# Layer entry after an expert loop: first weight panels taken from the loop's prefetch, the loop's last scatters moved in among the memory transposes

## The chip, the cores and the metric

The kernel runs on one core of one Trainium2 chip. The metric is the device time of one execution in microseconds (us); the time given for a kernel is the median of its runs. A profiled execution has a time of its own and a span, from the first to the last instruction that the profiler saw. The engines are named as in the profile: PE (TensorE, the matrix engine), DVE (VectorE), ACT (ScalarE), POOL (GpSimd), and SP (SyncE), which here only issues DMA transfers. Each runs its own instruction list in order, and they wait for one another by semaphores.

## What is computed

Two blocks follow each other on a sequence of 256 tokens of width 1024, all in float32. The first block ends in a layer whose feed-forward part is a mixture of 8 experts; its output is the residual `h` of the second block, two layers of a hybrid of attentions. Cut to what the change touches:

```python
def moe_swiglu(h, router, we_gate, we_up, we_down):      # end of the first block
    gates = ...                                          # softmax over the 2 best of 8 experts
    out = jnp.zeros_like(h)
    for e in range(N_EXPERTS):
        out = out + gates[..., e:e + 1] * swiglu(h, we_gate[e], we_up[e], we_down[e])
    return out

def hybrid_layer(x, mem, ...):                           # second block, twice
    h = rms_norm_2(x, g_mix)
    z = h @ w_in
    ...
    kv = (rms_norm_2(mem, g_mem) @ w_mkv)                # keys and values of the memory
    ...
    x = x + y @ w_o
    hm = rms_norm_2(x, g_mlp)
    return x + jnp.square(jax.nn.relu(hm @ w_up)) @ w_down
```

The 256 tokens are 2 tiles of 128. The 256 rows of `mem` do not depend on the first block.

## The kernel before, in words

**Panels.** All weights are streamed in panels of 128 x 1024 float32 (512 KB). Each product is made of three matmuls, so every panel is split: ACT writes the rounded part `whi` (`split_to`, line 556), DVE the rest `wlo` (line 1016). `whi` and `wlo` have 4 slots (`SLOTS`). Both engines keep a count of the panels split (`hi`, `lo`), PE a count of those used. The activations are split in the same way: PE transposes 4 tiles of 128 x 128 into one of two PSUM banks `TB` (`turn_group`, line 1898, called a turn below), ACT copies the bank out as the high part (line 591), DVE computes the low part (line 1064) and thereby frees the bank (`tfree`). Eight tiles in depth, four turns, make one operand for 256 tokens.

**The expert loop** (from about 480 us to 1468.5 us of the trace) does 8 jobs, one for each entry of a job table that DVE computes from the router (`tab`, lines 1509 to 1513); an entry is the number of an expert. SP streams a job's 84 panels from the array `wm` into a ring of 7 slots called `deep`; after the last panel of a job it loads the first 7 panels of the next job's expert, the "follower". The last job has a follower too: its table entry is the last expert, and nobody uses those 7 panels. A job ends with two chunks of 14 panels (`KE // 2`), which leave two halves of the job's output in PSUM; ACT and DVE split each into `outhi` and `outlo` (lines 865 and 1615, count `s_ol`). The output is scattered back to the tokens by 4 matmuls a half (`scatter`, line 2222, into the banks SC0 and SC1) and added to `h` by DVE (`add_scattered`, line 1572, two instructions a half, count `s_h`). In the loop this is done within the next job. For the last job it stands behind the loop.

**The entry of the hybrid layer** (`Walk(e, B)`, l = 0 and 1). The first chunk of a layer computes the memory's keys and values: 4 panels of 12 matmuls each, whose other operand is the transposed `mbuf` (the memory rows, scaled long before) in `chi` and `clo`. Four turns of `mbuf` feed it (`turn_rows`, `turned`). During its panels 2 and 3 the first two turns of `h` are made for the next chunk (`early`), with the other two to follow (`late`). The weights of this block come from an array `w2` into the ring `raw` of 4 slots. `raw` and `deep` lie on the same memory: slots 0 to 3 of `deep` are the 4 slots of `raw`, and slots 4 to 6 lie on `qkT`, which is written later in the layer.

What stands between the loop and the first panel, for l = 0: DVE adds both halves to `h`, then releases everything with six drains (`B.lo` for SP, `B.free`, `B.tfree`, `B.sfree`, `B.ofree`, `s_res` for PE), copies the norm gains (`n2`, line 1635, count `s_par`) and splits 3 panels before it comes to its part of the turns. PE waits for `s_res` and `s_par` before its first turn. SP waits for the 7 unused panels and for `B.lo`, then loads panel 0 of `w2`. ACT splits 3 panels, which wait for these loads, and only then copies out the first turn. `n2` is a table of 24 gains per layer; PE waits for `s_par` in the second layer too, and `chi` and `clo` lie on memory that the loop's `outhi` and `selT` and the feed-forward part's `fhi` and `flo` use.

Of the kernel before, what the change touches and what calls it, by code (L numbers as in the profile page):

```python
# [59 lines left out]
PER_TURN = {k: TURN * v for k, v in PER_JOB.items()}  # L60
PER_LAYER = dict(p=PANELS_B, g=30, t=16, n=2, h=0, s=16, a=6, r=16, v=8, o=6, u=6, k=10, va=0)
# [58 lines left out]
def build(nc, d):  # L120
    ctx = ExitStack()
    with ctx:
# [208 lines left out]
        class Walk:  # L331

            def __init__(self, e, s, chain=None):
                self.e, self.s, self.chain = e, s, chain
                self.key = "va" if chain is s.va else "vd"
                self.n = dict.fromkeys(PER_JOB, 0)
                self.split = 0
                self.ring = s.ring
                self.it, self.per = None, None

# [71 lines left out]
        def _(e):  # L412
# [41 lines left out]
            with e.Fori(0, turns) as it:  # L454
                for x in range(TURN):
                    expert = e.value_load(tab[0:1, bass.ds(it * TURN + (x + 1), 1)], min_val=0, max_val=NE - 1)
                    for p in range(DEEP, PANELS_M):
                        expert_panel(expert, p, p % DEEP, it * (TURN * PANELS_M) + (x * PANELS_M + p - DEEP + split))
                    follower = e.value_load(tab[0:1, bass.ds(it * TURN + (x + 2), 1)], min_val=0, max_val=NE - 1)
# [5 lines left out]
            with e.Fori(0, 2 * PANELS_B // SLOTS - 1) as k:  # L465
                for i in range(SLOTS):
                    e.wait_ge(B.lo, k * SLOTS + (SLOTS + i + 1))
                    e.dma_start(raw[:, i, :], d["w2"][bass.ds(k * SLOTS + (SLOTS + i), 1)].rearrange("a p n -> p (a n)")
                                ).then_inc(B.raw[i], 16)
# [72 lines left out]
        def _(e):  # L542
            act = nc.scalar.activation

            def split_to(w, target):

                while w.split < target:
# [5 lines left out]
                    e.wait_ge(loaded[slot], base if w.it is None else w.it * (16 * w.per["p"] // depth) + base)  # L553
# [451 lines left out]
        def _(e):  # L1005
            v = nc.vector

            def split_to(w, target):

                while w.split < target:  # L1010
                    p = w.split
                    w.split += 1
                    q = p + 1
                    slots, loaded, first = w.ring
                    e.wait_ge(w.s.hi, q if w.it is None else w.it * w.per["p"] + q)
                    v.tensor_tensor(wlo[:, p % SLOTS, :], slots[:, (p - first) % len(loaded), :], whi[:, p % SLOTS, :].bitcast(F32),  # L1016
                                    ALU.subtract).then_inc(w.s.lo, 1)
# [474 lines left out]
            for t in range(T):  # L1492
# [16 lines left out]
            w.link(v.tensor_tensor(tmp[:, :, 0:NE - 1], jobs_c[:, :, 0:NE - 1],  # L1509
                                   end.unsqueeze(1).to_broadcast(wide)[:, :, 0:NE - 1], ALU.is_ge))  # L1510
            v.tensor_scalar(R[:, 1041:1042], end[:, NE - 1:NE], TURN + 0.5, 1.0, ALU.is_gt, ALU.add)
            w.link(v.reduce_sum(R[:, 1042:1042 + MAXJOB], tmp[:, :, 0:NE - 1], axis=AX.X))
# [54 lines left out]
            def add_scattered(c, it, x):  # L1567

                e.wait_ge(s_scat, it * (2 * TURN) + (2 * x + c + 1))
                for t in range(T):  # L1570
                    x = h[:, t, c * 512:(c + 1) * 512]
                    i = v.scalar_tensor_tensor(x, SC[t][:, :], jobcur[:, 1, t:t + 1], x, ALU.mult, ALU.add)
# [48 lines left out]
            for c in range(2):  # L1621
                add_scattered(c, turns, 0)

            e.drain().then_inc(B.lo, SLOTS)
            e.drain().then_inc(B.free, 2)
            e.drain().then_inc(B.tfree, 2)
            e.drain().then_inc(B.sfree, 4)
            e.drain().then_inc(B.ofree, 2)
            e.drain().then_inc(s_res, 4)  # L1630
            w = Walk(e, B, B.vd)
            for l in range(2):
# [4 lines left out]
                split_to(w, LOOK)  # L1637
                turned(w, lambda k: n2[:, k:k + 1], (chi, clo))
# [173 lines left out]
        def _(e):  # L1812
# [405 lines left out]
            def scatter(c):  # L2218

                for t in range(T):  # L2220
                    for q, y in enumerate((outhi, outlo)):
                        i = mm(SC[t][:, :], selT[:, t, :], y[:, c, :], start=(q == 0), stop=(q == 1))  # L2222
# [57 lines left out]
            w = Walk(e, B)  # L2280
            for l in range(2):
                w.layer(l)
                e.wait_ge(s_par, l + 1)
                rows, ahead = turn_rows(w, mbuf, (A.nhn, 1)), early(w, h, (s_res, l * 4 + 3 + (l == 0)))

                def entry(panel):
                    rows(panel)
# [3 lines left out]
                chunk_tokens(w, chi, clo, FULL, before=entry)  # L2291
# [234 lines left out]
```

## Time and profile before

| | us |
|---|---|
| median of 3 runs | 2293.86 |
| lowest and highest | 2292.74, 2295.32 |
| the profiled execution's own time | 2297.4 |
| its span | 2295.5 |
| PE busy in the span | 2219.1 (97%) |
| DVE busy | 1726.7 (75%) |
| ACT busy | 1411.3 (61%) |
| mean of PE's granted clock | 0.984 of full |

The profile's page gives busy time by engine, a band of 40 slices, the chain of work that ended last, and the costliest groups. With PE busy 97% of the span, what is to be read is where PE is not busy, or busy at half its clock. The views with times of their own (the chain in order of time, the timeline of one engine, the table of stretches) count from the start of the span. Matmuls overlap: a row's length is that of one in the pipeline (0.39 us), while their starts stand 0.23 us apart.

### The profile page before, as it was taken

To read this page: it belongs to the slowest core of one execution; us is meant where nothing else is said; L and a number is where in the kernel's file an instruction comes from. 1 tells how busy PE (TensorE), PEld (TensorE's weight loads), DVE (VectorE), ACT (ScalarE), POOL (GpSimd) and SP (SyncE) were. 2 spreads that over 40 slices of the span, in tenths; PEclk is the share of its full clock that TensorE was granted. 3 is DMA by queue.
4 is the path that set the end of the run, shared out by engine and by line. 5 is a ranking of instruction groups with operands and counts; after the bars stand their busy time and mean duration, and the time that the engine had idled before them with its cause. 6 is when DMAs were issued, how large, how long until landed. Compare 5 with 4: busy or idle time off the path is not lost.

```text
span 2295.5 us, 36562 instructions
## 1 busy us (share of the span) xinstructions
PE 2219.1 (97%) x11818; PEld 1893.7 (82%) x11818; DVE 1726.7 (75%) x2308; ACT 1411.3 (61%) x1901; POOL 109.6 (5%) x113
## 2 busy tenths in 40 slices
PE   8999998999999999999999999799989999998998
PEld 7889986778888888888888888687879878887987
DVE  7856656588998989898989899666576546657654
ACT  4264445467887878777877778545545434564543
POOL 8300005000000000000000000000000000000000
PEclk9999998999999999999999999899999999999999
DMA  6235553269999999999999999754445555434554
GB/s 225 74 129 184 184 192 120 74 215 374 345 367 356 359 358 356 349 361 345 365 344 365 362 352 374 275 183 138 134 162 191 186 181 174 147 129 165 194 185 146
DMA packets 152640, 557.79 MB, mean 243 GB/s; under 512 B 16912, under 2 KB 17040, under 8 KB 152336
## 3 DMA queue, kind: packets, MB, share of 16 engines
q1 hardware_dynamic: 152032, 554.53, 67.5%
q8 instruction: 97, 1.59, 0.3%
q10 hardware_dynamic: 432, 1.02, 0.1%
q14 instruction: 79, 0.65, 0.1%
HBM read 554.44 MB, written 1.05 MB: 242 GB/s over the span
## 4 chain that ended last, share of the span: by engine, by line
PE 85%; issue 7%; DVE 4%; ACT 3%; DMA 1%; POOL 0%; DVEq 0%; ACTq 0%; SPq 0%; POOLq 0%
PE L L1830 59%; PE L L1883 10%; PE L L2316 5%; PE TB L1898 2%; PE L L1847 2%; PE SC L2061 1%; PE SC L2213 1%; PE L L2001 1%; PE SC L2222 1%; DVE wlo L1016 1%; ACT SMX L652 1%; PE SC L1968 1%; PE L L2111 1%; ACT whi L556 0%; DVE hn L1746 0%
## 5 line engine op out<-in xcount | busy, mean ns | idle before, releaser
L1016 DVE TENSOR_TENSOR wlo<-deep,whi 128x1024 fp32r<-128x1024 f32 x675 | 795.5, 1221 | 58.9 <-ACT whi L556 38.4
L556 ACT ACTIVATE whi<-deep 128x1024 fp32r<-128x1024 f32 x675 | 706.5, 1060 | 139.8 <-PE L L1830 135.5
L1016 DVE TENSOR_TENSOR wlo<-raw,whi 128x1024 fp32r<-128x1024 f32 x368 | 446.0, 1227 | 275.0 <-ACT whi L556 268.8
L556 ACT ACTIVATE whi<-raw 128x1024 fp32r<-128x1024 f32 x368 | 383.1, 1058 | 332.8 <-PE L L1830 191.0
L1830 PE MATMUL L<-whi,xhi 128*128 128x512 f32 (+1 forms) x1200 | 474.8, 396 | 8.7 <-DVE wlo L1016 4.8
L1830 PE MATMUL L<-whi,xlo 128*128 128x512 f32 (+1 forms) x1200 | 467.8, 390 | 0.0
L1830 PE MATMUL L<-wlo,xhi 128*128 128x512 f32 (+1 forms) x1200 | 467.7, 390 | 0.0
L1830 PEld LDWEIGHTS L<-whi,xhi 128*128 128x128 f32 x1200 | 226.7, 189 | 57.9 <-DVE wlo L1016 8.8
L1830 PEld LDWEIGHTS L<-whi,xlo 128*128 128x128 f32 x1200 | 226.5, 189 | 48.0
L1830 PEld LDWEIGHTS L<-wlo,xhi 128*128 128x128 f32 x1200 | 226.7, 189 | 44.7
L1830 PE MATMUL L<-whi,mhi 128*128 128x512 f32 x448 | 175.9, 393 | 0.0
L1830 PE MATMUL L<-wlo,mhi 128*128 128x512 f32 x448 | 174.5, 390 | 0.0
L1830 PE MATMUL L<-whi,mlo 128*128 128x512 f32 x448 | 174.4, 389 | 0.0
L1883 PE MATMUL L<-x2hi,whi 128*128 128x256 f32 x512 | 145.0, 283 | 0.0
L1883 PE MATMUL L<-x2hi,wlo 128*128 128x256 f32 x512 | 144.9, 283 | 0.0
L1883 PE MATMUL L<-x2lo,whi 128*128 128x256 f32 x512 | 144.9, 283 | 0.0
L1883 PE MATMUL L<-xhi,whi 128*128 128x256 f32 x448 | 127.4, 284 | 1.4 <-DVE xlo L1064 0.8
L1883 PE MATMUL L<-xlo,whi 128*128 128x256 f32 x448 | 126.8, 283 | 0.0
L1883 PE MATMUL L<-xhi,wlo 128*128 128x256 f32 x448 | 126.8, 283 | 0.0
L486 POOL TENSOR_TENSOR stat<-stat,halfneg 128x2 f32<-128x2 f32 (+3 forms) x18 | 21.6, 1198 | 2121.8 <-DVE stat L1038 1907.9
L1830 PE MATMUL L<-whi,fhi 128*128 128x512 f32 x280 | 109.3, 390 | 1.4 <-DVE wlo L1016 1.4
L1830 PE MATMUL L<-wlo,fhi 128*128 128x512 f32 x280 | 109.0, 389 | 0.0
(327 smaller groups left out, 3414.7 us busy)
## 6 DMA issues: line engine op xcount, KB each, us to landing
deep<-wm SPq DMA_DIRECT2D x679, 512.0 KB, 5.6
raw<-w SPq DMA_DIRECT2D x368, 512.0 KB, 4.0
mbuf<-mem SPq DMA_DIRECT2D x2, 1024.0 KB, 8.4
const<-const SPq DMA_DIRECT2D x1, 1312.0 KB, 7.7
out<-hn SPq DMA_DIRECT2D x2, 512.0 KB, 2.6
h<-x ACTq DMA_DIRECT2D x1, 512.0 KB, 4.9
h<-x SPq DMA_DIRECT2D x1, 512.0 KB, 4.8
mbuf<-gfin SPq DMA_DIRECT2D x1, 512.0 KB, 4.4
```

The lines of the kernel that those rows point to most:

```text
L556: act(whi[:, p % SLOTS, :], slots[:, slot, :], ACT.Copy).then_inc(w.s.hi, 1)
L652: ins = act(s, s, ACT.Exp, bias=top[:, 2 * x + t:2 * x + t + 1], scale=-1.0, accum_out=den[:, 2 * x + t:2 * x + t + 1])
L1016: v.tensor_tensor(wlo[:, p % SLOTS, :], slots[:, (p - first) % len(loaded), :], whi[:, p % SLOTS, :].bitcast(F32), ALU.subtract).then_inc( ...
L1830: i = mm(L[2 * (g % 2) + t][:, 0:width], x[:, k, row], y[:, slot, cols], start=(k == k0 and q == 0), stop=(k == k0 + n - 1 and q == 2))
L1847: i = mm(L[2 * (g % 2) + t][:, :], x[:, k, t * P:(t + 1) * P], y[:, slot, kk * 512:(kk + 1) * 512], start=(k == 0 and q == 0), stop=(k == ...
L1883: i = mm(out, x[:, slot, cols], y[:, k, :], start=(k == 0 and q == 0 and f % 2 == 0), stop=(k == KD - 1 and q == 2 and f % 2 == 1), skip_g ...
L1898: i = tr(TB[w.n["t"] % 2][:, c:c + P], src, ident)
L1968: ins = mm(bank(w, x)[:, t * S:t * S + c], qkT[half, qp, t * P:(t + 1) * P], key[half, 0:c], start=True, stop=True)
L2001: ins = mm(out(w, w.n["o"])[:, at:at + HD], PT[:, w.n["v"] % 2, x, kt * S + t * P:kt * S + (t + 1) * P], parts[j][2](x, kt), start=(j == 0 ...
L2061: ins = mm(SC[c % 2][:, f * S:(f + 1) * S], diag[2 * c + f][:, i, :], u[:, 2 * c + f, tap:tap + S], start=(i == 0), stop=(i == TAPS_PE - 1))
L2111: i = mm(L[2 * ((w.n["g"] + c) % 2) + t][:, :], x[:, k, row], y[:, slot, kk * 512:(kk + 1) * 512], start=(k == 0 and q == 0), stop=(k == K ...
L2316: i = mm(L[2 * (bank % 2) + t][:, :], x[:, k, t * P:(t + 1) * P], y[:, slot, kk * 512:(kk + 1) * 512], start=(k == 0 and q == 0), stop=(k ...
```

## The change

1. **Prefetch.** `w2` is appended to `wm` (`W2` is where it begins), and the job table counts over all 8 experts instead of 7, so that an entry behind the last job is 8: the follower of the last job is the first 7 panels of the hybrid block. SP no longer waits for `s_deep` nor loads panels 0 to 6 of `w2`; it goes on with panel 7 into `raw` slot 0 when panel 0 has been split. ACT and DVE read panels 0 to 6 from `deep` (`led`, `lead`).
2. **Final scatters.** `scatter(0)` goes into SC0 and SC1 as before but waits only for the first half of the output, `scatter(1)` into L2 and L3, two banks of the matmul accumulators. PE no longer waits for DVE's addition between them; it makes turns 0 and 1 of the memory rows between the two, and turn 2 behind them.
3. **Order on DVE and ACT.** DVE releases `B.lo`, `B.tfree` and one count of `B.free` straight behind the loop; then it splits one panel, does its part of a turn, and adds half 0; one more panel, one more turn, half 1; then the third panel and the turns 2 and 3; the other drains come behind. ACT splits one panel before each of the first three turns. ACT's first split now waits for `s_par`.
4. **Buffers and waits.** The memory rows' operand is written to `x2hi` and `x2lo` instead of `chi` and `clo`, in both layers; PE's wait for `s_par` is gone in both layers, ACT's wait for `s_h` as well.

```diff
-                    expert = e.value_load(tab[0:1, bass.ds(it * TURN + (x + 1), 1)], min_val=0, max_val=NE - 1)
+                    expert = e.value_load(tab[0:1, bass.ds(it * TURN + (x + 1), 1)], min_val=0, max_val=NE)
...
-            for i in range(DEEP):
-                e.wait_ge(s_deep[i], turns * (TURN * 16 * PANELS_M // DEEP) + 16)
-            panels(B, lambda i: d["w2"][i], SLOTS)
+            def later_panel(i, panel, split):
+
+                e.wait_ge(B.lo, split)
+                e.dma_start(raw[:, i, :], d["wm"][bass.ds(panel, 1)].rearrange("a p n -> p (a n)")).then_inc(B.raw[i], 16)
+
+            rest = 2 * PANELS_B - DEEP - SLOTS
+            for i in range(SLOTS):
+                later_panel(i, W2 + DEEP + i, SLOTS + i + 1)
...
ACT, layer entry
-            w = Walk(e, B, B.va)
+            w = Walk(e, B, B.va).led(turns)
...
-                split_to(w, LOOK)
                 e.wait_ge(s_par, l + 1)
-                turned(w, lambda k: n2[:, k:k + 1], chi)
-                e.wait_ge(s_h, turns * (2 * TURN) + 8)
+                e.wait_ge(w.s.used, w.at("p", SLOTS))
+                for q in range(4):
+                    if l == 0:
+                        split_to(w, min(q + 1, LOOK))
+                    turned_group(w, q, lambda k: n2[:, k:k + 1], x2hi)
...
DVE, behind the loop
-            for c in range(2):
-                add_scattered(c, turns, 0)
-
-
             e.drain().then_inc(B.lo, SLOTS)
-            e.drain().then_inc(B.free, 2)
             e.drain().then_inc(B.tfree, 2)
-            e.drain().then_inc(B.sfree, 4)
-            e.drain().then_inc(B.ofree, 2)
-            e.drain().then_inc(s_res, 4)
-            w = Walk(e, B, B.vd)
+            e.drain().then_inc(B.free, 1)
+            w = Walk(e, B, B.vd).led(turns)
...
-                split_to(w, LOOK)
-                turned(w, lambda k: n2[:, k:k + 1], (chi, clo))
+                for q in range(4):
+                    if l == 0:
+                        split_to(w, min(q + 1, LOOK))
+                    turned_group(w, q, lambda k: n2[:, k:k + 1], (x2hi, x2lo))
+                    if l == 0 and q < 2:
+                        add_scattered(q, turns, 0, (SC, L[2:4])[q])
+                        if q == 0:
+                            e.drain().then_inc(s_res, 3)
+                if l == 0:
+                    e.drain().then_inc(B.free, 1)
+                    e.drain().then_inc(B.sfree, 4)
+                    e.drain().then_inc(B.ofree, 2)
+                    e.drain().then_inc(s_res, 1)
...
PE, behind the loop
-            e.wait_ge(s_ol, turns * (2 * TURN) + 2)
+            e.drain().then_inc(B.used, SLOTS)
+            e.wait_ge(s_ol, turns * (2 * TURN) + 1)
             e.wait_ge(s_xj, turns * (TURN * 4) + 4)
             scatter(0)
-            e.wait_ge(s_h, turns * (2 * TURN) + 7)
-            scatter(1)
-
-
-            e.wait_ge(s_res, 4)
-            e.drain().then_inc(B.used, SLOTS)
+            w = Walk(e, B)
+            w.layer(0)
+            e.wait_ge(A.nhn, 1)
+            turn_group(w, mbuf, 0)
+            turn_group(w, mbuf, 1)
+            e.wait_ge(s_ol, turns * (2 * TURN) + 2)
+            scatter(1, L[2:4])
+            turn_group(w, mbuf, 2)
             e.drain().then_inc(B.rcopy, 2)
             e.drain().then_inc(B.pv, 2)
...
-                chunk_tokens(w, chi, clo, FULL, before=entry)
+                chunk_tokens(w, x2hi, x2lo, FULL, before=entry)
```

What stands in a row on the engines, printed from the built programs. In these rows `TB0` and `TB1` are the banks of the turns, `const` the identity, `b_thi` says that ACT has copied the turn out, `b_hi` that ACT has split the panel, `s_scat` that PE has scattered.

DVE from the end of the loop (line 1615, or 1637 after, splits the last half of the last job's output) in the kernel before:

```order
L1615 TENSOR_TENSOR outlo_64<-L0,outhi_63 128x512 [waits s_oh,a_free]
...
L1572 SCALAR_TENSOR_TENSOR h_54<-SC0,jobcur_102,h_54 128x512 [waits s_scat]
...
L1635 COPY n2_99<-small_95 128x24
L1016 TENSOR_TENSOR wlo_53<-raw_49,whi_52 128x1024 [waits b_hi,s_par]
L1016 TENSOR_TENSOR wlo_53<-raw_49,whi_52 128x1024 [waits b_hi] x2
L1064 SCALAR_TENSOR_TENSOR clo_68<-TB0,n2_99,chi_67 128x256 [waits b_thi]
```

And DVE from the same place in the changed kernel:

```order
L1637 TENSOR_TENSOR outlo_64<-L0,outhi_63 128x512 [waits s_oh,a_free]
...
L1650 COPY n2_99<-small_95 128x24
L1039 TENSOR_TENSOR wlo_53<-deep_51,whi_52 128x1024 [waits b_hi,s_par]
L1087 SCALAR_TENSOR_TENSOR x2lo_88<-TB0,n2_99,x2hi_87 128x256 [waits b_thi]
...
L1594 SCALAR_TENSOR_TENSOR h_54<-SC0,jobcur_102,h_54 128x512 [waits s_scat]
...
L1039 TENSOR_TENSOR wlo_53<-deep_51,whi_52 128x1024 [waits b_hi]
L1087 SCALAR_TENSOR_TENSOR x2lo_88<-TB1,n2_99,x2hi_87 128x256 [waits b_thi]
...
L1594 SCALAR_TENSOR_TENSOR h_54<-L2,jobcur_102,h_54 128x512 [waits s_scat]
```

The additions moved from ahead of the first panel's split to behind the first and the second turn, and the split reads `deep` instead of `raw`.

PE from the last job's scatters to the first matmul of the layer in the kernel before:

```order
L2222 MATMUL SC0<-outhi_63,selT_104 128x512 [waits s_xj]
...
L2222 MATMUL SC0<-outhi_63,selT_104 128x512 [waits s_h]
...
L1898 MATMUL TB0<-const_96,mbuf_75 128x128 [waits s_res,b_tfree,a_nhn,s_par]
...
L1898 MATMUL TB1<-const_96,mbuf_75 128x128 [waits b_tfree]
...
L1898 MATMUL TB0<-const_96,mbuf_75 128x128 [waits b_tfree]
...
L1830 MATMUL L0<-whi_52,chi_67 128x512 [waits b_lo,b_tfree,b_free]
```

And PE there in the changed kernel:

```order
L2248 MATMUL SC0<-outhi_63,selT_104 128x512 [waits s_xj]
...
L1924 MATMUL TB0<-const_96,mbuf_75 128x128 [waits b_tfree,a_nhn]
...
L1924 MATMUL TB1<-const_96,mbuf_75 128x128 [waits b_tfree]
...
L2248 MATMUL L2<-outhi_63,selT_104 128x512 [waits s_ol]
...
L1924 MATMUL TB0<-const_96,mbuf_75 128x128 [waits b_tfree]
...
L1856 MATMUL L0<-whi_52,x2hi_87 128x512 [waits b_lo,b_tfree,b_free]
```

The second scatter no longer waits for `s_h`, DVE's addition of the first half, and two turns stand ahead of it; the wait for `s_res` and `s_par` is gone.

## Rows read from the trace of the kernel before

**Rows 1.** Table of stretches: busy per engine (instructions), granted PE clock, DMA share, GB/s.
```profile
800.00:1000.00 200.00, 199.96 (x935) 166.15 (x934) 183.83 (x199) 158.31 (x188) 0.00 (x0) 1.00 0.95 355
...
1468.50:1502.30 33.80, 20.87 (x81) 16.18 (x81) 16.55 (x25) 12.21 (x20) 0.00 (x0) 0.70 0.47 163
...
1886.50:1903.50 17.00, 13.96 (x61) 11.53 (x62) 8.33 (x15) 6.03 (x12) 0.00 (x0) 0.80 0.19 66
```
**Rows 2.** Chain that ended last around the first entry: start us, us, what.
```profile
1437.10 31.41 PE L L1830 x138
...
1469.41 0.70 DVE outlo L1615
...
1470.22 1.20 PE SC L2222 x4
...
1472.91 2.09 PE SC L2222 x4
...
1477.44 6.02 DMA raw<-w
...
1483.48 1.06 ACT whi L556
...
1484.57 1.23 DVE wlo L1016
...
1486.63 1.12 PE TB L1898 x4
1487.75 5.07 PE L L1830 x12
1492.82 0.44 PE TB L1898 x4
1493.25 2.77 PE L L1830 x12
```
**Rows 3.** Timeline of DVE at the first entry: start, us, line, op, [idle before <-releaser].
```profile
1475.02 1.41 DVE L1572 SCALAR_TENSOR_TENSOR h<-SC,jobcur,h 128x512 f32<-128x512 f32 x2 [2.17 <-PE SC L2222]
1477.01 0.18 DVE L1635 COPY n<-small 128x24 f32<-128x24 f32 x1 [0.58 <-issue]
...
1494.16 0.88 DVE L1064 SCALAR_TENSOR_TENSOR clo<-TB,n,chi 128x256 fp32r<-128x256 f32 x2 [4.63 <-ACT chi L591]
```
**Rows 4.** Timeline of ACT at the first entry.
```profile
1487.79 0.84 ACT L591 ACTIVATE chi<-TB,n 128x256 fp32r<-128x256 f32 x2 [1.80 <-PE TB L1898]
```
**Rows 5.** Timeline of PE: first matmul of panel 0, first matmul of panel 4.
```profile
1487.40 0.78 PE L1830 MATMUL L<-whi,chi 128*128 128x512 f32 x1
...
1502.30 0.39 PE L1830 MATMUL L<-whi,xhi 128*128 128x512 f32 x1
```
**Rows 6.** Table of stretches, the first entry cut where the granted clock changes.
```profile
1468.50:1472.90 4.40, 1.18 (x4) 0.67 (x4) 3.00 (x4) 0.60 (x1) 0.00 (x0) 0.91 0.45 180
...
1486.60:1492.60 6.00, 5.97 (x16) 4.79 (x17) 1.64 (x4) 0.84 (x2) 0.00 (x0) 0.50 0.40 117
1492.60:1502.30 9.70, 9.70 (x50) 7.99 (x48) 5.84 (x9) 6.15 (x10) 0.00 (x0) 1.00 0.30 108
```
**Rows 7.** The loop's loads into `deep`: the last issues, and issue to landing.
```profile
1441.08 24.84 SPq L445 DMA_DIRECT2D deep<-wm  x19
...
DMA to landing us min/median/max: 3.1/5.6/7.4
```
**Rows 8.** Waits of ACT from 600 to 1440 us: total us, times, longest.
```profile
ACT whi L556 <- DMA deep<-wm: 3.8, 9, 0.7
```
**Rows 9.** Chain that ended last around the second layer's entry.
```profile
1888.16 0.19 DVE n L1635
...
1889.50 0.85 ACT chi L591 x2
...
1891.38 1.12 PE TB L1898 x4
1892.50 4.16 PE L L1830 x12
```
**Rows 10.** The same place in PE's timeline, and a stretch of it.
```profile
1888.39 1.84 PE L1898 MATMUL TB<-const,mbuf 128*128 128x128 f32 x8 [1.93 <-DVE n L1635]
...
1891.38:1895.40 4.02, 4.02 (x12) 3.35 (x13) 1.60 (x4) 0.84 (x2) 0.00 (x0) 0.50 0.02 4
```
**Rows 11.** Timeline of DVE, first instruction inside the expert loop.
```profile
479.26 1.22 DVE L1016 TENSOR_TENSOR wlo<-deep,whi 128x1024 fp32r<-128x1024 f32 x1 [1.14 <-issue]
```

More of the change, by code:

```diff
@@ L338, in __init__, with led @@
                 self.ring = s.ring
+                self.lead = None
                 self.it, self.per = None, None
+            def led(self, turns):
+                self.lead = turns * (16 * PER_TURN["p"] // DEEP) + 16
+                self.ring = (raw, self.s.raw, DEEP)
+                return self
             def at(self, kind, plus=0):
@@ L552, in split_to @@
                     slot, base = (p - first) % depth, 16 * ((p - first) // depth + 1)
-                    e.wait_ge(loaded[slot], base if w.it is None else w.it * (16 * w.per["p"] // depth) + base)
+                    if w.lead is not None and p < DEEP:
+                        slots, slot = deep, p
+                        e.wait_ge(s_deep[p], w.lead)
+                    else:
+                        e.wait_ge(loaded[slot], base if w.it is None else w.it * (16 * w.per["p"] // depth) + base)
                     q = p + 1
@@ L1014, in split_to @@
                     slots, loaded, first = w.ring
+                    slot = (p - first) % len(loaded)
+                    if w.lead is not None and p < DEEP:
+                        slots, slot = deep, p
                     e.wait_ge(w.s.hi, q if w.it is None else w.it * w.per["p"] + q)
-                    v.tensor_tensor(wlo[:, p % SLOTS, :], slots[:, (p - first) % len(loaded), :], whi[:, p % SLOTS, :].bitcast(F32),
+                    v.tensor_tensor(wlo[:, p % SLOTS, :], slots[:, slot, :], whi[:, p % SLOTS, :].bitcast(F32),
                                     ALU.subtract).then_inc(w.s.lo, 1)
@@ L2216, in gather, with scatter @@
                         i.then_inc(s_gat, 1)
-            def scatter(c):
+            def scatter(c, banks=SC):
                 for t in range(T):
                     for q, y in enumerate((outhi, outlo)):
-                        i = mm(SC[t][:, :], selT[:, t, :], y[:, c, :], start=(q == 0), stop=(q == 1))
+                        i = mm(banks[t][:, :], selT[:, t, :], y[:, c, :], start=(q == 0), stop=(q == 1))
                 i.then_inc(s_scat, 1)
@@ L2268, in _ @@
                 w.end("pgt")
-            e.wait_ge(s_ol, turns * (2 * TURN) + 2)
+            e.drain().then_inc(B.used, SLOTS)
+            e.wait_ge(s_ol, turns * (2 * TURN) + 1)
             e.wait_ge(s_xj, turns * (TURN * 4) + 4)
             scatter(0)
-            e.wait_ge(s_h, turns * (2 * TURN) + 7)
-            scatter(1)
-            e.wait_ge(s_res, 4)
-            e.drain().then_inc(B.used, SLOTS)
+            w = Walk(e, B)
[6 more added lines that the diff above has]
+            turn_group(w, mbuf, 2)
             e.drain().then_inc(B.rcopy, 2)
             e.drain().then_inc(B.pv, 2)
-            w = Walk(e, B)
             for l in range(2):
-                w.layer(l)
-                e.wait_ge(s_par, l + 1)
-                rows, ahead = turn_rows(w, mbuf, (A.nhn, 1)), early(w, h, (s_res, l * 4 + 3 + (l == 0)))
+                if l == 1:
+                    w.layer(l)
+                    for q in range(3):
+                        turn_group(w, mbuf, q)
+                ahead = early(w, h, (s_res, l * 4 + 3))
                 def entry(panel):
-                    rows(panel)
+                    if panel == 1:
+                        turn_group(w, mbuf, 3)
+                    e.wait_ge(w.s.tfree, w.at("t", max(panel - 1, 0)))
                     if panel == 3:
```

22 lines of the change are left out of this document (11 added, 11 removed).

## The prediction

> **What bounds the kernel now.** I read the table of stretches first. In the expert loop PE is busy for all of its time at full clock, and so nothing can be won there except by less PE work [rows 1]. In the 33.8 us after it, 1468.5 to 1502.3, PE is busy 20.9 us at a mean clock of 0.70, and in the 17 us at the second layer's entry 14.0 us at 0.80 [rows 1]. The change touches these two places. The chain of waits, read second, tells what fills the first: the split of the last half, scatter, addition, scatter, addition, then the load of a panel (6.02 us), its split on ACT (1.06) and DVE (1.23), a turn, and panel 0 at half clock (5.07 where panel 1 takes 2.77) [rows 2]. Panel 0 starts at 1487.40 and panel 4, the first of the next chunk, at 1502.30 [rows 5]. From panel 4 on PE's work and order are the same in both kernels, so the gain of this entry is how much earlier panel 4 starts. The six drains and the copy of the gains take from 1476.43 (1475.02 + 1.41) to 1477.19 [rows 3].
>
> **The load goes.** The 7 panels that the loop fetches last are now the ones needed. Their last issue is near 1465.9 (1441.08 + 24.84) and a load of this ring lands within 7.4 us [rows 7], by 1473.3 at worst; panel 0, six issues of 1.38 us earlier (24.84 over 18), is there when the loop ends. SP has nothing on the path any more: panel 7 is asked for when panel 0 is split, and is needed after seven panels of 2.77 us [rows 2]. Seven loads of 256 are saved, which PE does not notice. The longer count in the job table adds 17 elements to two small DVE instructions; I cost it at nothing.
>
> **The new chain, step by step.** T = 1468.51 is the end of the loop's matmuls (1437.10 + 31.41), and DVE ends the last split at 1470.11 (1469.41 + 0.70) [rows 2]. Both stay.
> - DVE then has three drains and the copy. Six drains took 0.58 us; three take 0.3 to 0.6, with the copy 0.18 [rows 3]: 1470.8.
> - ACT waits for this copy (`s_par`, the new wait) with the split of panel 0 and all later panels behind it, and DVE in turn waits for ACT. 1.06 us: 1471.9. Its copy of turn 0 takes 0.84 [rows 4]: 1472.75. PE has made turns 0 and 1 by then, from 1470.4 on, and both scatters.
> - DVE splits panel 0 (1.23) to 1473.2 and does turn 0 (0.88 [rows 3]) to 1474.1. This releases PE's turn 2; the first matmul followed such a turn's start by 0.77 us (1487.40 against 1486.63) [rows 2, 5]. Panel 0 starts at 1474.9, against 1487.4: 12.5 us earlier.
> - From here DVE is the slow one, as the additions now lie among its turns. It goes on: addition 1.41, a drain 0.1, split 1.23, turn 1 0.88, to 1477.7; addition 1.41, split 1.23, turn 2 0.88, to 1481.25; turn 3 0.88, four drains 0.4, split 1.23, first turn of `h` 0.88, to 1484.6; split and second turn of `h` 2.1, to 1486.7.
> - PE: panel 1 needs turn 1, panel 2 turn 2, panel 3 the first turn of `h`, panel 4 the second. Each takes a turn of 0.44 and 2.77 [rows 2].
>
> **The clock decides the last us.** In the first entry before, the clock was full through the first scatter (1.20 us for 4) and half in the second (2.09 for 4), after PE had been idle 1.7 and 1.5 us [rows 2, 6]. At the second entry it was half at the first turns after an idle 1.93 us [rows 10]. In the changed kernel PE is idle some 0.9 us ahead of the turns and 1.8 us behind the second scatter, much like that, so I take the half clock (1.2 GHz of 2.4) for the start of panel 0. It came back 6.0 us after PE resumed at the first entry [rows 6] and 4.0 us after at the second [rows 10]. With 4.0 from 1474.1, panel 0 has 7.5 matmuls at 0.43 us and 4.5 at 0.23, and ends at 1479.1; with 6.0 it ends at 1480.1. Then panels 1, 2 and 3 follow at 3.2 us each (PE is now later than DVE): 1482.4, 1485.6, 1488.8, or 1483.3, 1486.5, 1489.7. Panel 4 starts at 1488.8 to 1489.7 instead of 1502.3: 12.6 to 13.5 us won. I take **13.1**.
>
> **The second layer.** PE's turns no longer wait for the gains. What is left is that ACT starts when the gains are copied, at 1888.4 (1888.16 + 0.19), instead of 1889.50 behind PE's first turn [rows 9]: **1.1 us**. The additions that end the layer stay ahead of the copy. Bounds: nothing, if ACT is slow to start, and 2.5 us if the turns, now straight behind the last matmul, also save the slow clock of panel 0 (4.16 against 2.77 us, 1.4 [rows 2, 9]). Other buffers (`x2hi` for `chi`) have the same shape, and the tables of waits show no reader of them in these stretches: zero. Nothing in the 384 us behind each entry changes; all loads there are covered, so I let the gain pass whole to the end.
>
> **Sum.** 13.1 + 1.1 = 14.2. The profiled execution of 2297.4 us would become 2283.2. It stood 3.5 us over the median of the runs, 2293.86, so the median becomes **2279.7**, a gain of 0.62%.
>
> **Rivals.**
> - *The clock stays full.* Then DVE's chain sets the pace: panel 1 starts at 1478.1, panel 2 at 1481.7, panel 3 at 1485.0, panel 4 at 1487.8. That is 14.5 us, with 1.1 to 2.5 in the second layer 15.6 to 17: 2276.9 to 2278.3. For it: PE has turns and a scatter in a stretch where it idled before. Against it: the two idle times of the same length that did end in half clock. Chance 0.25.
> - *Leaving the loop stalls.* Behind the loop ACT and DVE had slack before that would hide a slow first instruction: DVE waited 1.35 us for the scatter, ACT far longer. Now both stand on the path at once. At the loop's entry DVE's first instruction came 1.14 us late with nothing to wait for [rows 11]. One such stall on the chain gives 13.1 - 1.1 = 12.0, on two engines in a row 10.8: medians of 2280.8 to 2282.0. Chance 0.15.
> - *The clock stays half through the whole chunk.* If the shorter idle times leave it low while PE waits for DVE, the panels take 5.1 us and turns 0.9: 1474.9 + 5.1 + 3 x 6.0 = 1498.0. A gain of 4.3 and 1.1, a median of 2288.5. Against it: at half clock PE is the slower one and idles nowhere, as when the clock came back before. Chance 0.06.
> - *The loop's stream slows (slower than before).* The loop draws 355 GB/s with the DMA engines 95% taken [rows 1] from an array that is now longer and lies elsewhere. PE never waited, and ACT only 3.8 us in 840 [rows 8], so there is little slack. Below the 355 that PE uses, each per cent costs 10 us of the 1000 of the loop; 2% lower gives 2293.9 - 14.2 + 20 = 2299.7, and it decides from 1.4% on. Against it: same sizes, same strides, same queue. Chance 0.02.
> - *The prefetch is not what is used*, say because the loads land late. Panel 0 would wait; they would have to be 7 us later than any in the loop. 0.01. The rest, 0.51, is the forecast.
>
> **How the numbers follow.** The likeliest case gives 2279.7, with its own range 2278.5 to 2281.5. The range of 8 in 10 takes in the full clock with a good second layer (2276.9, less 1.4 us, about the spread of the runs, 2292.74 to 2295.32 around 2293.86) and the stalls, with as much above them for unmeasured drains and waits: 2275.5 to 2285.5. A measurement of this kernel can tell about 0.2% (4.6 us) from no change; faster means below 2289.3. All cases but the stream and part of the half clock are there: faster 0.94, same 0.04, slower 0.02.
>
> **What would show it.** In the changed kernel's trace: no wait of ACT's first splits for a DMA; ACT's split of panel 0 within 0.1 us of the gains' copy, and that near T + 2.3; panel 0 at T + 6.4 (before T + 18.9) and panel 4 between T + 19.3 and T + 21.2 (before T + 33.8); the scatters' and panel 0's matmuls at 0.23 or 0.43 us apart tell the clock. A gap at the exit shows as idle time of DVE or ACT with nothing waited for. In the second layer ACT's first copy stands 0.1 us behind the gains' copy. The loop should keep its length, and the rest too. I am wrong if DVE is not the one that PE waits for in panels 1 to 3 at full clock, or if the time comes back later in the layer, as waits for panels 7 to 10, whose loads start further apart than before.

## The result, and the profile after

| | before | changed |
|---|---|---|
| median of 5 runs, us | 2293.98 | 2279.27 |
| lowest and highest | 2292.74, 2296.36 | 2275.37, 2284.33 |
| profiled execution, its span | 2297.4, 2295.5 | 2279.27, 2277.5 |
| mean of PE's granted clock in it | 0.984 | 0.992 |

The changed kernel takes 0.9936 of the time before, 95% interval 0.9921 to 0.995, 14.7 us less at the medians. Two more comparisons of the same two kernels gave 0.9922 (0.9903 to 0.9942) and 0.9932 (0.9918 to 0.9946). Its times spread over 9 us, though, and those of the kernel before do so too where it ran more often (18 runs beside after_again: 2288.50 to 2297.61 us). Why is told below, since it also explains why the changed kernel's profiled execution is 18.1 us shorter than that of before and not 14.7.

The stretch at the first entry, from the table of stretches (columns as in [rows 1]), answers to the second row of [rows 1]:

```profile
1466.64:1487.50 20.86, 17.93 (x80) 14.06 (x81) 16.17 (x25) 11.89 (x20) 0.00 (x0) 0.92 0.39 137
```

20.9 us instead of 33.8, with PE busy 17.9. The chain that ended last there (start, us, what) answers to [rows 2]:

```profile
1466.66 0.61 ACT outhi L883
...
1467.54 0.69 DVE outlo L1637
...
1468.53 0.02 DVEq L1643
...
1468.81 0.19 DVE n L1650
...
1469.16 1.07 ACT whi L574
...
1470.33 0.72 DVE wlo L1039
...
1472.40 0.66 PE TB L1924 x4
1473.05 0.37 issue
1473.42 4.60 PE L L1856 x12
1478.02 0.44 PE TB L1924 x4
1478.45 2.78 PE L L1856 x12
...
1484.88 5.50 PE L L1856 x24
```

No load, no scatter and no addition is in it. The loop's matmuls end at T = 1466.64; panel 0 starts at T + 6.8, and panel 4, in the middle of the last row, at 1487.63 = T + 21.0. Before, by the same reading, it was T + 33.9 (1499.69 + 2.75 against 1468.51). PE's timeline shows where it waits and where the clock changes:

```profile
1468.79 1.06 PE L1924 MATMUL TB<-const,mbuf 128*128 128x128 f32 x8 [0.63 <-DVEq L1644]
...
1472.40 0.66 PE L1924 MATMUL TB<-const,mbuf 128*128 128x128 f32 x4 [1.61 <-DVE x2lo L1087]
1473.42 0.74 PE L1856 MATMUL L<-whi,x2hi 128*128 128x512 f32 x1 [0.37 <-issue]
...
1476.09 0.63 PE L1856 MATMUL L<-whi,x2hi 128*128 128x512 f32 x1
...
1477.15 0.40 PE L1856 MATMUL L<-whi,x2hi 128*128 128x512 f32 x1
```

Between the turns and turn 2 lies the second scatter, like the first at full clock (4 matmuls in 1.2 us). The clock falls after the 1.6 us of idle time ahead of turn 2. Turn 2 itself takes the 0.66 us that it takes below where the clock stays full, and the first slow matmul is that of 1473.42. It is back near 1476.8, 4.4 us after PE resumed; the rows of 0.63 us are of 1.2 GHz, those of 0.40 of 2.4. The second layer's entry, in the chain of waits, answers to [rows 9]:

```profile
1870.15 1.42 DVE h L1810 x2
...
1871.80 0.19 DVE n L1650
...
1872.01 0.85 ACT x2hi L609 x2
...
1873.89 0.66 PE TB L1924 x4
1874.54 2.73 PE L L1856 x12
...
1884.14 5.50 PE L L1856 x24
```

PE's first turns are gone from it, and panel 0 takes 2.73 us instead of 4.16. I call D the start of DVE's last addition of the first layer (1870.15, before 1886.50). Panel 4 starts at D + 16.7, before at D + 19.75.

The execution thus falls into five pieces that can be laid beside those of any other trace: the start up to T, T to panel 4, panel 4 to D, D to panel 4 of the second layer, and the rest. Between before and changed they differ by 1.9, 12.9, 1.5, 3.0 and -1.4 us, 18.0 in all.

### The profile page after: what moved, and what is told of

It is laid out like the page before. It is cut to its first block, busy times and chain, and to the rows that moved or that the text cites. A ratio compares the mean times of both kernels' runs of the same rounds, so it can differ in the third digit from the quotient of the medians.

```text
span 2277.5 us, 36522 instructions
## 1 busy us (share of the span) xinstructions
PE 2210.7 (97%) x11818; PEld 1887.9 (83%) x11818; DVE 1726.5 (76%) x2308; ACT 1411.2 (62%) x1901; POOL 111.2 (5%) x113
## 4 chain that ended last, share of the span: by engine, by line
PE 85%; issue 7%; DVE 4%; ACT 3%; DMA 0%; POOL 0%; DVEq 0%; ACTq 0%; POOLq 0%
PE L L1856 59%; PE L L1909 10%; PE L L2348 5%; PE TB L1924 2%; PE L L1873 2%; PE SC L2087 1%; PE SC L2239 1%; PE L L2027 1%; DVE wlo L1039 1%; ACT SMX L670 1%; PE SC L2248 1%; PE L L2137 1%; PE SC L1994 1%; ACT whi L574 0%; DVE hn L1772 0%
## 5 line engine op out<-in xcount | busy, mean ns | idle before, releaser
L1039 DVE TENSOR_TENSOR wlo<-deep,whi 128x1024 fp32r<-128x1024 f32 x682 | 804.6, 1220 | 60.6 <-ACT whi L574 39.6
L574 ACT ACTIVATE whi<-deep 128x1024 fp32r<-128x1024 f32 x682 | 714.1, 1061 | 141.6 <-PE L L1856 135.2
L1039 DVE TENSOR_TENSOR wlo<-raw,whi 128x1024 fp32r<-128x1024 f32 x361 | 437.3, 1226 | 269.6 <-ACT whi L574 263.7
L574 ACT ACTIVATE whi<-raw 128x1024 fp32r<-128x1024 f32 x361 | 375.8, 1058 | 320.5 <-PE L L1856 190.1
```

Source lines behind the costliest of these rows:

```text
L574: act(whi[:, p % SLOTS, :], slots[:, slot, :], ACT.Copy).then_inc(w.s.hi, 1)
L1039: v.tensor_tensor(wlo[:, p % SLOTS, :], slots[:, slot, :], whi[:, p % SLOTS, :].bitcast(F32), ALU.subtract).then_inc(w.s.lo, 1)
```

## The experiments

**The changed kernel twice more.** No edit.

> The changed kernel once more, for the spread of its times (2275.37 to 2284.33 us in five) and a second trace. Theory A: the times differ by what clock is granted where PE is idle for moments, at the two entries and elsewhere; then the trace has panel 0 of the first layer anywhere between 2.8 and 5.1 us long, the loop and the distance from the end of the loop's matmuls to panel 0 (6.8 us in the first trace) stay within 0.3 us, and the time is 2275 to 2285 again. Theory B: the loads or a stall at the end of the loop vary; then that distance varies by microseconds.

> The changed kernel a third time, beside e4_again for a direct comparison. From the end of the loop's matmuls to panel 4 either 21.0 us (panel 0 takes 4.6, half clock) or 19.4 (3.0, full clock, as in e5_par_wait, which had the same code there); from DVE's last addition of the first layer to panel 4 of the second 16.7 or 18.4. Nothing between.

The medians were 2275.33 (six runs, 2274.26 to 2284.28) and 2277.79 us (six, 2275.05 to 2284.62). Theory B is out: in the three traces the way from T to panel 0 and its length differ by no more than 0.1 us. So this entry does not spread the times of these three; what does lies elsewhere. The first entry, in the chain of waits of after_again:

```profile
1472.25 4.58 PE L L1856 x12
...
1483.70 5.50 PE L L1856 x24
```

Panel 4 is at T + 21.0 in all three (T = 1465.47 here, 1468.83 in after_third), with panel 0 4.57 to 4.60 us long. The second entry is D + 16.7, 16.8, or, in after_again, 18.4, where panel 0 had half clock. The other pieces, whose work is the same in every kernel of this study, have few values, not a spread: panel 4 to D is 382.5 to 382.6 or 383.8 to 384.1 us in all fourteen traces, the last piece 389.1 to 389.3, 390.6 to 390.8, or, in e7_dve_more, 391.2. For the first pair the place can be seen in the table of stretches of PE (stretch, length, PE busy, granted clock, DMA share, GB/s), first of the changed kernel, then of after_again, both 160 us behind panel 4:

```profile
1647.63:1667.63 20.00, 14.39 (x65) 1.00 0.49 165
```

```profile
1646.45:1666.45 20.00, 14.39 (x59) 0.91 0.50 157
```

PE idles 5.3 to 5.6 of 20 us here in every trace. In eight of the fourteen, that of before among them, the granted clock of this stretch is 0.91, and these are the eight with 383.8 to 384.1 us from panel 4 to D; the other six have 1.00 and 382.5 to 382.6. So the fall costs 1.3 to 1.6 us, and what decides whether it comes is not shown. I call that a toss. T itself is anywhere between 1462.8 and 1469.1, with the same code before it but for the job table, and here too the clock goes with it: between 300 and 400 us and between 400 and 480 us it is 0.97 and 0.98 in the trace with the earliest T (e6_once_fill2), 0.93 and 0.95 in that with the latest (e7_dve_more). Such places are the spread of the times as far as the traces show it; I did not cut the part before T into single places.

**The prefetch alone.** The array, the job table, SP's loads and the reading of `deep` as in the changed kernel; order, banks and buffers as before:

```diff
+            w = Walk(e, B, B.vd).led(turns)
...
             for c in range(2):
                 add_scattered(c, turns, 0)
...
                 split_to(w, LOOK)
                 turned(w, lambda k: n2[:, k:k + 1], (chi, clo))
```

> The prefetch alone: job table, array, SP's loads and the reading of panels 0 to 6 from the deep ring as in the changed kernel, the order on DVE, ACT and PE, the banks and the buffers as before. Theory A (the additions, and not only the load, hold the entry up): panel 0 starts some 14.6 us behind the end of the loop's matmuls instead of 18.9 (gains copied at +8.7, ACT splits three panels to +11.9, turn 0 on ACT and DVE to +13.8), all at half clock, panel 4 at about +29.5 instead of +33.8: 4.3 us won, 2289.7 us. Rival: the load of 6.0 us was the whole of it, with the additions hidden: then this alone wins 9 us or more.

Ratio 0.9973 (0.9963 to 0.9984), or 6 us less; the medians are 2288.65 against 2295.48 us in these runs. Its chain of waits:

```profile
1468.26 0.60 ACT outhi L883
...
1472.64 2.09 PE SC L2242 x4
...
1478.07 3.50 DVE wlo L1037 x3
...
1483.52 3.70 PE L L1850 x12
...
1494.09 5.50 PE L L1850 x24
```

The load is gone, but scatter, addition, scatter, addition and now DVE's three splits (3.50 us) fill most of its place. Panel 4 is at T + 28.6 (T = 1468.24): 5.3 us won, where 4.3 were expected; the clock came back during panel 0 (3.70 us). The load's length was not the whole of it.

**Everything but the prefetch.** Order, banks, buffers and waits as in the changed kernel, the old follower and the old loads:

```diff
-            w = Walk(e, B, B.vd).led(turns)
+            w = Walk(e, B, B.vd)
...
+            for i in range(DEEP):
+                e.wait_ge(s_deep[i], turns * (TURN * 16 * PANELS_M // DEEP) + 16)
+            panels(B, lambda i: d["w2"][i], SLOTS)
```

> The other parts alone: order, banks, buffers and waits as in the changed kernel, but the last follower is the last expert again, and SP loads panel 0 of the hybrid block only when the loop's splits and its 7 unused loads are done. Theory A: the load starts near +3 us behind the loop's matmuls instead of +8.9, panel 0 is split by +11 and PE starts it at +12.5 to +13 (half clock), panel 4 at +27 to +28: 6 us at the first entry and 1.1 to 2.9 at the second layer's, 2285 to 2287 us. The two parts then give less alone (4.3 + 6) than together (12.9 at the first entry), since either one leaves the other's work on the path. Rival: the parts add up, the load's 6 us and the rest each by itself.

Ratio 0.9954 (0.9937 to 0.9971), 2282.84 us. The chain of waits:

```profile
1465.39 6.57 DMA deep<-wm
...
1472.10 3.30 DMA raw<-w
...
1480.27 5.43 PE L L1851 x12
...
1492.56 5.49 PE L L1851 x24
```

Here the chain runs back through the unused load of the seventh panel: SP had to see it land at 1471.97 before it could ask for panel 0. In the kernel before DVE's additions hid that. With T = 1468.31 panel 4 is at T + 27.0: 6.9 us won, and D + 16.7 at the second entry, 3.0 won. At the first entry the parts give 5.3 and 6.9 us alone, and 12.9 together. So they come close to adding up. The expectation of a clear excess (4.3 + 6 against 12.9) was mostly two sizes that I had set too low; what is left over is 0.7 us. These figures contain whatever clock panel 0 happened to get (it is 3.70 us long in e1_prefetch_only, 5.43 here, 4.60 in the changed kernel). Counted only to the first matmul of panel 0 in the chains, they are 4.0 and 7.3 alone and 12.5 together, and 1.2 is left over. The order, the banks and the dropped waits are one parcel here; only the banks are taken apart further, in e8_same_banks.

**Filling PE's idle time.** 6, then 3 matmuls of the identity by a constant behind the second scatter:

```diff
             scatter(1, L[2:4])
+            warm(3, L[0])
             turn_group(w, mbuf, 2)
```

> The changed kernel with 6 matmuls of 128 x 256 more (the identity by a constant, into bank L0, whose content is overwritten) between the second scatter and turn 2, where PE idled 1.6 us; each takes some 0.22 us at full clock. Theory A: the half clock of panel 0 (4.60 us instead of 2.77) comes from this idle time; filled, panel 0 runs at full clock, DVE's chain becomes the pace, panel 4 starts 1.5 to 1.9 us earlier than the changed kernel's +20.9, 2277.5 us median, and the spread of the times shrinks. Rival: the clock falls anyway, or the entry is DVE's already, and the time stays within 0.3 us.

> The changed kernel with 3 filler matmuls (shown as 6 instructions, 1.3 us) instead of 6 between the second scatter and turn 2. The 6 took 2.6 us where 1.6 were idle and held turn 2 up by 1 us. Theory A (the half clock of panel 0 comes from the idle time ahead of it): panel 0 starts at +6.8 behind the loop's matmuls as in the changed kernel but takes 2.8 to 3.0 us instead of 4.6, and panel 4 starts at +19.0 to +19.4 instead of +20.9. Theory C (DVE's chain with the two additions in it becomes the pace as soon as the clock is full): panel 2 or 3 waits for DVE, some 0.3 us of the 1.8 are lost, +19.4. Rival: too little to hold the clock, and +20.9 stays.

The 6 were too many. Each such float32 matmul is two instructions of 0.22 us, which I had counted as one, and the chain shows them holding turn 2 up, by 1 us (T = 1466.69, panel 4 at T + 20.2, panel 0 3.01 us long):

```profile
1470.84 2.59 PE L L1918 x12
1473.43 0.44 PE TB L1924 x4
```

With 3, turn 2 is where it was, and panel 0 has the full clock:

```profile
1471.77 0.66 PE TB L1924 x4
...
1472.81 3.00 PE L L1856 x12
...
1482.68 5.50 PE L L1856 x24
```

T = 1466.02, panel 4 at T + 19.4, 1.6 us earlier than in the three traces without the filler. One trace is no proof that the filler did it, because e5_par_wait below has the full clock at this place without any; all traces together are counted behind the next experiment. The medians, 2279.43 (ratio 0.9935) and 2279.9 us (0.9933), show nothing of it; the spread was 2.6 us with 6 fillers (six runs) and 9.5 with 3 (six runs), and so that part of the expectation stays open.

**Panels 0 to 2 split once.** In the changed kernel the loop's last splits already run 3 panels ahead into its follower, which is this block now, and the layer splits them again. Here they are counted as done:

```diff
 ACT
+            e.drain().then_inc(B.hi, LOOK)
             w = Walk(e, B, B.va).led(turns)
+            w.split = LOOK
 DVE
-            e.drain().then_inc(B.lo, SLOTS)
+            e.drain().then_inc(B.lo, SLOTS + LOOK)
...
+            w.split = LOOK
```

> The changed kernel, but the first three panels of the hybrid block are not split a second time. The expert loop's last splits already ran ahead into them (its follower is this block now), into the same slots 0 to 2 of whi and wlo; the counts are set as if the new layer had split them. Theory A (ACT's and DVE's splits of panels 0 to 2 are on the path): ACT starts with turn 0 when the gains are copied (+2.4), DVE's part of turn 0 ends near +4.3 instead of +5.7, PE idles 0.3 us there instead of 1.6, so the clock stays full; panel 4 near +17 instead of +20.9, a median some 3.9 us under the changed kernel's (0.9913 of the kernel before instead of 0.993). Rival: the adds or PE's turns bound it, and at most the 1.2 us of the first split are won.

> e4_split_once again: panel 4 at +18.4 behind the loop's matmuls, as in its first trace (not the +17 expected there: PE is the pace from panel 0 on, 3.0 + 3 x 0.44 + 3 x 2.77 = 12.6 us, and panel 0 starts at +5.8, since turn 0 is made only at +2.2 when tfree is released, and a turn costs 1.0 us to the next matmul). Against the changed kernel on the same chip 1.0 us (its clock full) to 2.6 us (half) less; the median 1 to 3 us lower, at the edge of what the runs can tell.

Chain of waits of the first of the two:

```profile
1468.50 0.64 PE TB L1927 x4
...
1469.24 0.85 ACT x2hi L609 x2
...
1471.12 0.66 PE TB L1927 x4
...
1472.15 3.01 PE L L1859 x12
...
1482.02 5.50 PE L L1859 x24
```

Panel 4 at T + 18.4 in both (T = 1466.35 in the first), not +17. The step that failed is that ACT would start when the gains are copied. It waits for PE's turn 0, which cannot begin before DVE's release of `tfree` and starts at T + 2.15. Then 0.66 and 0.37 us lie between the start of turn 2 and the first matmul. The clock stayed full in both. PE's timeline has the idle time ahead of turn 2, 0.6 us where the changed kernel has 1.6:

```profile
1471.12 0.66 PE L1927 MATMUL TB<-const,mbuf 128*128 128x128 f32 x4 [0.62 <-DVE x2lo L1089]
```

Taken over all traces with this order and the prefetch but e8_same_banks, panel 0 had the full clock in all five in which this idle time was 0.6 us or filled (e3_fill, e3b_fill3, e4_split_once, e4_again, e6_once_fill2), and in one of the five in which it was 1.6 us (e5_par_wait; not in the three of the changed kernel, nor in e7_dve_more below). That speaks for the idle time having a part in it, and shows that it does not decide alone. The medians were 2276.49 (ratio 0.9917, 0.9904 to 0.9929) and 2276.82 us (0.9929, 0.9916 to 0.9942), the latter beside 2277.79 of the changed kernel on the same chip. The traces show 1.0 to 2.6 us less at this entry; the times cannot tell that from nothing.

**The second entry.** PE's wait put back; and, on top of the single split, 6 fillers between turns 1 and 2 of the second layer:

```diff
 e5
                     w.layer(l)
+                    e.wait_ge(s_par, l + 1)
                     for q in range(3):
 e6
+                    e.wait_ge(w.s.free, w.at("g", 1))
+                    warm(6, L[0])
                     turn_group(w, mbuf, 2)
```

> The changed kernel with PE's wait for the copied gains put back ahead of the second layer's turns; the buffers stay x2hi and x2lo. Theory A: it is this wait that made the second entry shorter. From the end of the first layer's matmuls to panel 4 it took 19.8 us before, 17.0 and 18.4 in the two traces of the changed kernel; here 19.6 to 19.9 again, with ACT's first copy 1.1 us behind the gains' copy instead of 0.02, and panel 0 4.1 to 4.4 us long. Rival: the other buffers did it; then it stays at 17 to 18.4.

> As e4_split_once, and at the second layer's entry 6 filler matmuls into bank L0 between turns 1 and 2 (2.6 us, where PE idled 2.9). Theory A: panel 0 of the second layer is at full clock in every execution (2.8 us instead of 2.7 in one trace and 4.3 in the other), so the median falls by another 0.8 us or so and the spread of the times by 1.6. Rival: the spread comes from elsewhere (the attentions, the first block), and stays at 9 us.

e5_par_wait took 2283.55 us (ratio 0.9946, 0.9933 to 0.996). Its second entry:

```profile
1866.89 1.42 DVE h L1810 x2
...
1868.78 0.97 PE TB L1924 x4
...
1869.86 0.85 ACT x2hi L609 x2
...
1872.85 4.20 PE L L1856 x12
...
1883.92 5.50 PE L L1856 x24
```

Panel 4 at D + 19.8, as before the change, with the new buffers: the wait is what mattered. Of the 3.0 us, ACT's earlier start is 1.1. The other 1.9 is the clock, in turn 2 (0.66 us against 1.12) and panel 0 (2.73 against 4.16), and only in executions where it holds; in after_again, where it fell, 0.2 is left. The clock was half here in all three traces in which PE waits for the gains (before, e1_prefetch_only, this one) and in four of the ten in which it does not and has no filler. At the first entry this kernel had 3.01 us for panel 0 and panel 4 at T + 19.4 (T = 1463.39), with the same code as the changed kernel: the clock's fall there is a toss as well, four to one in the five traces with 1.6 us of idle time. e6_once_fill2 has D + 16.8 with panel 0 at full clock, as six of the ten traces without the filler have, and a median of 2276.63 us (2271.47 to 2277.19), ratio 0.9914 (0.9902 to 0.9927). Its spread was 5.7 us in five runs; against the medians of e4_split_once and e4_again (2276.49 and 2276.82) nothing can be told, and the expectation stays open.

**More work on DVE, and the old banks.**

```diff
 e7
                         if q == 0:
+                            for t in range(T):
+                                v.scalar_tensor_tensor(mkv[:, t, :], SC[t][:, :], jobcur[:, 1, t:t + 1],
+                                                       h[:, t, 512:D], ALU.mult, ALU.add)
                             e.drain().then_inc(s_res, 3)
 e8
             e.wait_ge(s_ol, turns * (2 * TURN) + 2)
-            scatter(1, L[2:4])
+            e.wait_ge(s_h, turns * (2 * TURN) + 7)
+            scatter(1)
```

> The changed kernel with two more DVE instructions of an addition's kind and size (1.4 us together, into mkv, which is written over later) behind the first addition. Theory D (what the prediction held for full clock: DVE with its additions is the pace of panels 1 to 3): panel 1 waits for DVE by about 0.8 us at full clock, the entry takes 20.2 instead of 19.4. Theory P (PE is the pace from panel 0 on): DVE has turn 1 ready at +9.2, or +10.6 here, and panel 0 ends at +9.8 at full clock and +11.4 at half; at half clock nothing is lost and the entry stays at 21.0, and the panels 2 and 3 wait in neither.

> The changed kernel with the second scatter back in SC0 and SC1, so that PE waits for DVE's first addition ahead of it, all else (prefetch, the order, one panel at a time) kept. Theory A: the addition ends at +7.0, turn 2 is made behind the second scatter at about +8, panel 0 starts near +9 instead of +6.8 with PE idle 5 us before it, so at half clock for sure: panel 4 at +23.0 to +23.6 instead of 19.4 to 21.0, the median 2.3 to 4 us over the changed kernel's. Rival: the banks are worth nothing, since DVE is what PE waits for there anyway.

The timeline of DVE in e7_dve_more, then its chain of waits:

```profile
1476.01 1.40 DVE L1660 SCALAR_TENSOR_TENSOR mkv<-SC,jobcur,h 128x512 f32<-128x512 f32 x2
...
1478.67 0.87 DVE L1087 SCALAR_TENSOR_TENSOR x2lo<-TB,n,x2hi 128x256 fp32r<-128x256 f32 x2
```

```profile
1475.86 4.58 PE L L1859 x12
1480.43 0.44 PE TB L1927 x4
...
1487.29 5.50 PE L L1859 x24
```

Turn 1 is ready at 1479.54, T + 10.5, and panel 0 ends at 1480.43. PE waits for nothing there, and panel 4 is at T + 21.0 (T = 1469.07) as without the extra work. This trace had half clock, so the other half of the expectation, 0.8 us at full clock, was not tried. The median, 2281.69 us (ratio 0.994, 0.9928 to 0.9952), is 3.9 over the changed kernel's of the same runs, yet the intervals overlap, and at the entry the trace has no place for it. The profiled execution is slow in pieces that the edit does not touch: its T is the latest of all, and its last piece the longest.

e8_same_banks in PE's timeline:

```profile
1473.55 0.80 PE L2248 MATMUL SC<-outhi,selT 128*128 128x512 f32 x1 [3.86 <-DVE h L1594]
...
1476.85 0.48 PE L1856 MATMUL L<-whi,x2hi 128*128 128x512 f32 x1 [0.37 <-issue]
```

PE waits 3.9 us for the addition; panel 4 is at T + 23.0, and 2282.72 us are 4.9 over the changed kernel (ratio 0.9949, 0.9936 to 0.9962, against 0.9932, 0.9918 to 0.9946, so here too the intervals overlap and the trace is the better evidence). The banks of their own, with the wait that they save, are worth 2.0 us of the entry against the traces where panel 0 was at half clock, and 3.6 against that of e5_par_wait, where it was at full clock as here. "At half clock for sure" was wrong: the scatter ran at half (2.08 us for 4), and the clock was back for panel 0.

## Why the prediction was right, point by point

Forecast 2279.7 us, measured 2279.27; the gain 14.2 against 14.7.

- *The chain behind the loop* held step by step. Gains copied at T + 2.36 (T + 2.3 said), turn 0 done on DVE at T + 5.7 (T + 5.6), panel 0 at T + 6.8 (T + 6.4). Of the 0.4 us, 0.3 lie between turn 2 and the next matmul: I took 0.77, and it was 0.66 + 0.37. The 0.37 us are most likely PE's own drains (`B.rcopy`, `B.pv`), which the new order puts between turn 2 and panel 0 and for which the sum had no term. They stand in all twelve traces with that order, at the first entry, and neither in before and e1_prefetch_only, where the drains lie ahead of the turns, nor at any second entry, where there are none.
- *The drains* were sized rightly only with the end of the loop left out. Before, the six drains filled the 0.58 us ahead of the copy [rows 3]. Now three drains stand in 0.59 us, but half of it, from the end of the split at 1468.23 to the first drain at 1468.53, is the end of the loop on DVE, which before lay within its 1.35 us of waiting for the scatter; the three drains are the other 0.28, the low end of the 0.3 to 0.6 that I gave them.
- *The clock at the first entry*: taken as half for panel 0 and back within 4.0 to 6.0 us, it was back after 4.4. Panel 4 T + 21.0, forecast 20.3 to 21.2. The gain of this entry was 12.9, forecast 13.1. That it was the half clock is luck in part: in one of the five traces with the same idle time it was full.
- *The rival of the full clock* (panel 4 at T + 19.3) is no other case but the other outcome of the same toss: 19.4 in e5_par_wait and e3b_fill3. Its number came out by another way than the one named, as the next point says.
- *DVE as the slow one* was wrong, by the first sign that the prediction itself had named. From panel 0 on PE is the pace, at either clock (the chain of e5_par_wait has only PE in it from turn 2 on, at full clock): 3.0 + 3 x 0.44 + 3 x 2.77 is 12.6 us, and 6.8 + 12.6 is the 19.4 measured. I had DVE's times right (turn 1 at T + 9.2, measured 9.2), but PE started panel 0 0.4 us later and took 3.0 for it instead of 2.77, and so never waited; e7_dve_more shows 1.4 us more on DVE hidden at half clock. The other sign, that the time comes back later in the layer, did not come: from panel 4 to D it is 384.1 us before and 382.5 or 384.1 in the changed kernel.
- *The second entry* was undersized: 1.1 forecast with a bound of 2.5, measured 1.4 and 3.0. The mechanism was the one named, ACT's start (1.14 us earlier); the other term, the clock, I left out of the sum and put in the bound, for panel 0 alone (1.4), and it is 1.9 with turn 2. e5_par_wait, where both are lost again, confirms that they come from the wait.
- *The stall on leaving the loop* did not come. DVE's copy stood 0.59 us behind the last split, three drains included, which leaves 0.30 us for the exit, where the rival had 1.14.
- *The stream of the loop* kept its rate: 356 and 361 GB/s in two stretches of 200 us, 355 before [rows 1]; ACT waited 2.5 us for it, before 3.8 [rows 8].
- *The profiled execution* came out at 2279.27 and not 2283.2. Of the 3.9 us, 2.0 come from the pieces outside the change (1.9 + 1.5 - 1.4), 1.9 from the second entry. That the median agreed within 0.4 us is luck within a spread of 9 us; the 12.9 and 1.4 or 3.0 us at the two entries are the firmer evidence for the forecast.

## What to carry to other kernels

A prefetch that must fetch something at the end of a loop may as well fetch what comes next; but behind it stands the next queue of waits: a load of 6 us taken off the path gave 5.3 us alone and 6.0 once the additions and the second scatter had left the path too, and this other part gave 6.9 by itself. When a wait is taken off, count the granted clock with it, as two outcomes: at both entries 1.6 us came or went with it, after the same idle time. And if a kernel's traces differ by more than the edit, cut them at marks that every version has and compare piece by piece: here the pieces that the change touches repeat within 0.1 us for the same clock where the times spread by 9.

## What the runs showed of the hardware

- The same idle time ends in half clock in one execution and not in the next: at the first entry 4 times in 5 (1.6 us idle), at the second 4 times in 10 (2.9 us idle), at a place 160 us behind the entry 8 times in 14 (granted clock 0.91 against 1.00). Each costs 1.3 to 1.6 us.
- The clock that falls can be back before it matters: in e8_same_banks it was half for a scatter at 1473.55 and full for the matmul at 1476.85, with turns of 0.85 us between.
- Transposes run at the granted clock like matmuls: 4 took 1.12 us at 1.2 GHz and 0.44 at 2.4 GHz [rows 2, 6].
- Two drains on PE between a turn and the next matmul go with 0.37 us in which it waits for nothing, in twelve traces of twelve; without them the gap is not there.
- A load that nobody reads can be on the path: in e2_order_only that of the last unused panel, 6.57 us, delayed the first useful one.
